# Transformer block on one core: the residual reaches the output by copies and accumulating transfers, operand sums get four places, and the steps of the last down stage are reordered

## The reference

```
h = rms_norm(x, pre_ffn_norm) * (1.0 + sc2) + sh2
u = h @ w_up;  a, b = split(u, 2)
a = causal 3-tap convolution of a, + conv_b
y = (gelu(a) * b) @ w_down            # 5504 -> 2048
out = x + g2 * rms_norm(y, post_ffn_norm)
```

## Time and profile before

| | us |
|---|---|
| median of 3 runs (lowest, highest) | 2706.27 (2702.97, 2706.83) |
| the profiled execution: its time | 2704.7 |
| its span, first to last event | 2703.1 |
| TensorE busy | 2629.2 (97%) |
| VectorE busy | 2077.8 (77%) |
| ScalarE busy | 1158.3 (43%) |
| GpSimd busy | 210.0 (8%) |

### The profile page before, as it was taken

How to read it: one execution, slowest core, us unless ns; L and a number is a source line. 1 busy time by engine, 2 the same in 40 slices (tenths; PEclk the granted TensorE clock), 3 DMA queues, 4 the chain that set the end, 5 groups by cost and what they waited for, 6 DMA issues and landing times.

```text
span 2703.1 us, 40800 instructions
## 1 busy us (share of the span) xinstructions
PE 2629.2 (97%) x14114; PEld 2208.5 (82%) x14114; DVE 2077.8 (77%) x3029; ACT 1158.3 (43%) x1553; POOL 210.0 (8%) x334
## 2 busy tenths in 40 slices
PE   5999999999999999999989999999999998999997
PEld 5788888888788888887878888888888887888886
DVE  7956676666766666626657999999999998888988
ACT  4344444444622222223254444444444444454544
POOL 0030000000000000002200111111111111111000
PEclk8999999999999999999989999999999999999999
DMA  9932322333277777736743665656565566888894
GB/s 362 335 113 85 87 82 81 86 86 86 68 221 217 217 217 217 217 96 234 270 148 94 168 163 128 163 135 159 140 152 147 145 154 218 299 295 310 312 330 149
DMA packets 477847, 485.64 MB, mean 180 GB/s; under 512 B 24603, under 2 KB 381234, under 8 KB 475040
## 3 DMA queue, kind: packets, MB, share of 16 engines
q1 hardware_dynamic: 442160, 384.87, 47.1%
q0 software_dynamic: 25664, 94.93, 11.8%
q10 hardware_dynamic: 9904, 4.26, 0.6%
HBM read 428.28 MB, written 34.75 MB: 171 GB/s over the span
## 4 chain that ended last, share of the span: by engine, by line
PE 90%; DVE 4%; DMA 2%; ACT 2%; issue 1%; SPq 1%; DVEq 0%; POOL 0%; ACTq 0%; POOLq 0%
PE acc_bank L849 14%; PE acc_bank L851 14%; PE acc_bank L850 14%; PE acc_bank L1280 8%; PE acc_bank L1284 4%; PE bank_pb L1280 3%; PE bank_tb L1280 3%; PE bank_ta L1280 3%; PE two_banks L1280 3%; PE two_banks L849 2%; PE two_banks L851 2%; PE two_banks L850 2%; PE two_banks L1284 1%; PE bank_pb L1284 1%; PE bank_tb L1284 1%
## 5 line engine op out<-in xcount | busy, mean ns | idle before, releaser
L840 DVE TENSOR_TENSOR w_lo<-raw,w_hi 128x1024 fp32r<-128x1024 f32 x215 | 263.0, 1224 | 371.5 <-ACT w_hi L834 371.4
L834 ACT CAST w_hi<-raw 128x1024 fp32r<-128x1024 f32 x215 | 225.4, 1049 | 541.6 <-PE acc_bank L851 379.4
L849 PE MATMUL acc_bank<-h_hi,w_hi 128*128 128x512 f32 x1124 | 447.4, 398 | 6.4 <-DVE h_lo L2008 6.4
L851 PE MATMUL acc_bank<-h_hi,w_lo 128*128 128x512 f32 x1124 | 439.1, 391 | 0.0
L850 PE MATMUL acc_bank<-h_lo,w_hi 128*128 128x512 f32 x1124 | 438.8, 390 | 0.0
L849 PEld LDWEIGHTS acc_bank<-h_hi,w_hi 128*128 128x128 f32 x1124 | 211.6, 188 | 50.3 <-issue 6.5
L851 PEld LDWEIGHTS acc_bank<-h_hi,w_lo 128*128 128x128 f32 x1124 | 211.5, 188 | 45.4
L850 PEld LDWEIGHTS acc_bank<-h_lo,w_hi 128*128 128x128 f32 x1124 | 211.8, 188 | 41.8
L1280 PE MATMUL acc_bank<-h_pair,s_hi 128*128 128x512 f32 x640 | 160.3, 392 | 0.0
L1994 DVE SCALAR_TENSOR_TENSOR acc<-raw,csil,acc 128x512 f32<-128x512 f32 x180 | 135.1, 751 | 11.0 <-DMA raw<-in_w_mod_dram 6.5
L1280 PEld LDWEIGHTS acc_bank<-h_pair,s_hi 128*128 128x128 f32 x640 | 115.1, 189 | 20.6
(11 more groups left out here) (730 smaller groups left out, 6355.3 us busy)
## 6 DMA issues: line engine op xcount, KB each, us to landing
raw<-in_w_in_dram SPq DMA_DIRECT2D x148, 512.0 KB, 4.0
raw<-in_w_mod_dram SPq DMA_DIRECT2D x96, 512.0 KB, 4.5
raw<-in_w_ffn_up_dram SPq DMA_DIRECT2D x92, 512.0 KB, 4.9
raw<-in_w_ffn_down_dram SPq DMA_DIRECT2D x86, 512.0 KB, 5.9
raw_odd<-in_w_ffn_up_dram SPq DMA_DIRECT2D x80, 512.0 KB, 5.1
raw_more<-in_w_ffn_down_dram SPq DMA_DIRECT2D x63, 512.0 KB, 6.0
mods_low<-in_w_mod_dram SPq DMA_DIRECT2D x32, 512.0 KB, 10.1
raw<-in_w_out_dram SPq DMA_DIRECT2D x32, 512.0 KB, 4.4
```

Of the source, the lines that this page charges most:

```text
L834: act.copy(w_pair(g, gp)[0][:], raw[n % RAW][:]).then_inc(hi_ready, 1)
L840: dve.tensor_tensor(w_l[:], raw[n % RAW][:], w_h[:].bitcast(F32), ALU.subtract).then_inc(lo_ready, 1)
L849: pe.matmul(o, stat[0], mov[0], start=start, stop=False)
L851: return pe.matmul(o, stat[1], mov[0], start=False, stop=stop)
```

## The change

- The residual no longer passes through SBUF. Where `x2_again` was loaded, GpSimd's queue copies `x2_scr` into `out`, DRAM to DRAM, four rows of 1 MB. Finished rows or half rows are then added to `out` by transfers that accumulate (`accum_op`), on GpSimd's queue. SyncE's final stores go.
- `finish_half` with its residual becomes a multiplication by rms alone: six half rows on ScalarE (`scale_half`), two on VectorE.
- The operand sums have four places in both stages (`u_place`): `op_group_u(g)` waits for the store of group g - 4, and stage 1 loads up to four ahead. The loads wait for the landing of the load before them on the same semaphore.
- `LEFT_B` gets a place of its own (`left_b`), `LEFT_B_AT` goes from 7 to 3 and `LEFT_B_AGAIN` from 12 to 6. The steps of `third_stage`, the squares and the first two roots move to earlier j; the products by the gain all come before the end of stage 3.

The core of the diff (parts left out are marked):

```diff
-LEFT_B_AT = 7
-LEFT_B_AGAIN = 12
+LEFT_B_AT = 3
+LEFT_B_AGAIN = 6
...
-        def u_made(g):
-            return y2[:, 2 + g % 2, 0:512].rearrange("p (k t) -> p k t", k=2)[:, 0:group_tiles(g)[1], :]
-
-        def u_again(g):
-            return y2[:, 2 + g % 2, 512:1024].rearrange("p (k t) -> p k t", k=2)[:, 0:group_tiles(g)[1], :]
+        def u_place(g):
+            c = g // 2 % 2 * 512
+            return y2[:, 2 + g % 2, c:c + 512].rearrange("p (k t) -> p k t", k=2)[:, 0:group_tiles(g)[1], :]
...
-            for i in range(TT + 1):
-                r = ROW_ORDER[min(i, TT - 1)]
-                n, cols = (2 * i + 2, slice(0, D)) if i < TT - 1 else (TT + i, slice((i - TT + 1) * PIECE, (i - TT + 2) * PIECE))
-                sp.wait_ge(out_ready, READY_0 + n)
-                sp.dma_start(out_rows[r][:, cols], y2[:, r, cols]).then_inc(out_stored, 16)
-            sp.wait_ge(out_stored, OUT_0 + 16 * (TT + 1))
...
+            def scale_half(n, half, y):
+
+                i = ROW_ORDER[n]
+                act.wait_ge(scale_ready, SCALE_0 + n + 1)
+                A_(y, y, ACT.Identity, scale=rms[:, i:i + 1]).then_inc(out_ready, 1)
...
+                    if st == 3 and j == 15:
                         y_rms(0)
                         y_rms(1)
...
+                    if st == 3 and j in (18, 19):
+                        n = j - 18
+                        act.wait_ge(b_weighed, 3 + n)
+                        scale_half(n, 0, quarter_row("a1", n))
+                        scale_half(n, 1, quarter_row("b1", n))
...
-                if g > 1:
-                    dve.wait_ge(u_stored[g % 2], U_STORED_0 + 16 * (g // 2))
+                if g > 3:
+                    dve.wait_ge(u_stored[g % 2], U_STORED_0 + 16 * (g // 2 - 1))
...
-            def finish_half(i, half, y):
-                cols = slice(half * PIECE, half * PIECE + PIECE)
-                STT(y2[:, i, cols], y, rms[:, i:i + 1], x2_again[:, i, cols], ALU.mult, ALU.add).then_inc(out_ready, 1)
+            def finish_half(i):
+                dve.wait_ge(scale_ready, SCALE_0 + 3 + i)
+                y = quarter_row("b0", i)
+                TS(y, y, rms[:, i:i + 1], None, ALU.mult).then_inc(quarter_step, 1)
...
-                if j in (4, 5):
                     dve.wait_ge(bank_kept, KEPT_0 + 12)
-                    dve.wait_ge(quarter_step, QUARTER_0 + 2)
-                    for b in (2 * j - 8, 2 * j - 7):
+                    for b in (2 * j - 4, 2 * j - 3):
                         add_bank("p5", 1, "a1", "a1", b)
...
+                if j in (5, 7):
+                    less_second("b0", (j - 5) // 2)
+                if j in (6, 7):
                     dve.wait_ge(quarter_step, QUARTER_0 + 6)
-                    for b in (2 * j - 22, 2 * j - 21):
+                    for b in (2 * j - 12, 2 * j - 11):
                         add_bank("left1", 1, "b1", "b1", b, ALU.subtract)
...
-            for i in ROW_ORDER:
-                pool.dma_start(x2_again[:, i, :], x2_scr[i]).then_inc(back_landed, 16)
+            for i in range(TT):
+                pool.dma_start(out_rows[i], x2_scr[i]).then_inc(back_landed, 16)
+
+            def add_to_out(r, cols, y):
+                pool.dma_start(out_rows[r][:, cols], y, accum_op=ALU.add).then_inc(back_landed, 16)
+
             pool.wait_ge(back_landed, 64)
+            for n in range(2):
+                pool.wait_ge(out_ready, READY_0 + 2 * n + 2)
+                add_to_out(2 + n, slice(0, D), y2[:, 2 + n, :])
+            for i in range(2):
+                pool.wait_ge(quarter_step, QUARTER_0 + 11 + i)
+                if i == 0:
+                    pool.wait_ge(out_ready, READY_0 + 5)
+                    add_to_out(0, slice(0, PIECE), weighed_row[:, 0, :])
+                    add_to_out(0, slice(PIECE, D), y2[:, 0, PIECE:D])
+                else:
+                    add_to_out(1, slice(PIECE, D), y2[:, 1, PIECE:D])
+                    pool.wait_ge(out_ready, READY_0 + 6)
+                    add_to_out(1, slice(0, PIECE), weighed_row[:, 1, :])
+            pool.wait_ge(back_landed, 64 + 16 * 6)
```

More of the change, by code:

```diff
@@ L1922, in _ @@
-                    if st == 3 and j == 17:
+                    if st == 3 and j in (8, 9):
+                        act.wait_ge(bank_added, 8 + 2 * (j - 8) + 2)
+                        square_row(j - 8, "b1", j - 8, 4 * (j - 6) + 2)
+                    if st == 3 and j in (10, 11):
+                        act.wait_ge(quarter_step, QUARTER_0 + j - 1)
+                        square_row(j - 8, "a1", j - 10, 4 * (j - 8) + 1)
+                    if st == 3 and j in (12, 13):
+                        act.wait_ge(bank_added, 12 + 2 * (j - 12) + 2)
+                        square_row(j - 8, "b0", j - 12, 4 * (j - 12) + 2)
@@ new lines, in square_last @@
+            def square_last(i, part):
+                act.wait_ge(y_added, 2 * i + part + 1)
+                act.wait_ge(y2_sq, SQ_0 + 6 + 2 * i + part)
+                A_(op_sum[:, 0].rearrange("p a b -> p (a b)"), y2[:, i, part * 512:part * 512 + 512], ACT.Square,
+                   accum_out=ssg[:, 4 * i + part:4 * i + part + 1]).then_inc(y2_sq, 1)
+            square_last(0, 0)
+            square_last(0, 1)
+            y_rms(2)
+            square_last(1, 0)
+            act.wait_ge(b_weighed, 8)
@@ L1937, in _ @@
+            scale_half(2, 0, weighed_row[:, 0, :])
+            square_last(1, 1)
+            y_rms(3)
+            act.wait_ge(b_weighed, 10)
+            scale_half(3, 0, weighed_row[:, 1, :])
         @block.vector
@@ new lines, in third_stage @@
+                if j in (9, 10):
+                    dve.wait_ge(quarter_step, QUARTER_0 + 8)
+                    for b in (2 * j - 18, 2 * j - 17):
+                        add_bank("left0", 1, "b0", "b0", b, ALU.subtract)
+                if j == 11:
+                    dve.wait_ge(gain_landed, 32)
+                    for i in range(2):
+                        dve.wait_ge(y2_sq, SQ_0 + 1 + i)
+                        weigh_row("b1", i)
+                if j in (12, 13):
+                    i = j - 12
+                    dve.wait_ge(y2_sq, SQ_0 + 3 + i)
@@ L2733, in third_stage @@
                     weigh_row("a1", i)
+                    sum_row(2 + i, 1, 3 + i)
                 if j in (14, 15):
[L2735 to L2742, removed]
-                    root_of(0)
-                    dve.wait_ge(back_landed, 64)
-                    dve.wait_ge(b_weighed, 1)
-                    finish_half(2, 0, quarter_row("a1", 0))
@@ L2819, in _ @@
                         third_stage(j)
[L2821 to L2824, removed]
             def finish_last(b):
@@ L2983, in store_u @@
                     pool.wait_ge(u_stored[g % 2], U_STORED_0 + 16 * (g // 2))
-                pool.dma_start(u_scr[g][:, 0:n, :], u_made(g)).then_inc(u_stored[g % 2], 16)
+                pool.dma_start(u_scr[g][:, 0:n, :], u_place(g)).then_inc(u_stored[g % 2], 16)
             def load_u(st, g):
                 n = group_tiles(g)[1]
-                pool.wait_ge(u_stored[g % 2], U_STORED_0 + 16 * (g // 2 + 1))
-                if g >= 2:
-                    if st == 1:
-                        pool.wait_ge(op_step, op_step_no(1, g - 2, 1))
-                    else:
-                        pool.wait_ge(op_lo_ready, op_no(2, 0, g - 2))
-                pool.dma_start((u_again(g), op_sum[:, g % 2, 0:n, :])[st - 1], u_scr[g][:, 0:n, :]).then_inc(u_landed[g % 2], 16)
+                over = max(n for n in range(OP_GROUPS) if n % 4 == g % 4) if st == 1 else g
+                pool.wait_ge(u_stored[over % 2], U_STORED_0 + 16 * (over // 2 + 1))
+                landed = g // 2 + (st == 2) * ((OP_GROUPS + 1 - g % 2) // 2)
+                if landed:
+                    pool.wait_ge(u_landed[g % 2], U_LANDED_0 + 16 * landed)
+                if st == 1 and g >= 4:
+                    pool.wait_ge(op_step, op_step_no(1, g - 4, 1))
+                if st == 2 and g >= 2:
+                    pool.wait_ge(op_lo_ready, op_no(2, 0, g - 2))
+                pool.dma_start((u_place(g), op_sum[:, g % 2, 0:n, :])[st - 1], u_scr[g][:, 0:n, :]).then_inc(u_landed[g % 2], 16)
             def bring_act(g):
@@ L3021, in _ @@
                 pool.wait_ge(x2_stored[i], 16)
-            load_u(1, 0)
-            load_u(1, 1)
+            for g in range(4):
+                load_u(1, g)
             pool.wait_ge(grow_stored, 32)
@@ L3027, in _ @@
                 store_sum(j)
-                if j % 2 == 0 and j // 2 + 2 < OP_GROUPS:
-                    load_u(1, j // 2 + 2)
+                if j % 2 == 0 and j // 2 + 4 < OP_GROUPS:
+                    load_u(1, j // 2 + 4)
             pool.wait_ge(op_lo_ready, op_no(1, 1, OP_GROUPS - 1))
```

62 lines of the change are left out of this document (22 added, 40 removed).

## The result

Over 12 runs of each the changed kernel takes 2710.68 us (2709.22 to 2712.35) and the one before 2705.47 (2702.97 to 2707.95): ratio 1.0021, 95% interval 1.0012 to 1.0029. The change costs 5.2 us; the forecast was 6.1 us less, 2700.2, and 2710.7 lies above its range. The profiled execution took 2709.22 us, with a span of 2707.6, 4.5 us more than before's 2703.1.

A forecast was written before the change was run, and what follows sets the result against it. TensorE holds 90% of the chain, so time could come only from its waits and the stretch after its last matmul. Stage 0 -6.4, stall +0.5, end -0.2: -6.1 from 2706.27 gives 2700.2 us, range 2698.3 to 2702.5.

The forecast's parts named there:

- The end: After the last matmuls: engines finish 6 us earlier, but accumulating transfers take this back, leaving 0.2 us gained.
- T: Start of the four kept pieces near the kernel's end, 2677.90 in the trace before; times of the end count from it.
- the one of the other side: Rival at the end: read, add and write in DRAM do not overlap, 15.6 us more, 2715.8, slower; 13%.
- Stage 0: Four places remove VectorE's wait for a store; TensorE's gap shrinks to 2.1 us, clock stays 1.00; 6.4 us gained.
- `LEFT_B` again: Stage 3: TensorE waits for VectorE's additions to banks 2 and 3, a stall of 0.5 us, bounds 0 and 2.7.
- The copy: Stage 3: copying into out costs nothing; a rival had it starve the weights, 4 us, 2704.2; 4%.
- The last bank: At the end: piece 20 is 0.4 us late where 1.2 was lost before, so the bank is full at T + 11.4.
- The price a: Time of an accumulating transfer into DRAM at the end: 2.86 us per 512 KB, bounds 1.28 and 4.14.
- both rivals of a dearer accumulation: At the end: 3.3 to 4.4 us per 512 KB, 2708.9 at 4.14, 13%; or 5.0 us without overlap, 2715.8, 13%.
- the one of a = 1.28: Rival at the end: accumulation costs no more than a store, engines set the end at T + 18.9, 2694.1; 12%.
- The last landing: At the end: row 0 asked for at T + 11.8, four halves take 11.4 us, last lands at T + 25.0.
- The signal that I named: Sign of a wrong prediction: last engine idle more than 11 us before the end, meaning a larger price a.

The follow-up runs named there:

- no_pool_drain: The changed kernel with its block closed without GpSimd's drain, GpSimd still waiting for the landings; 2703.84 us, ratio 0.9995 to the kernel before.
- pool_waits_last: The kernel before with one wait more: GpSimd too waits until SyncE's output stores have landed; 2711.17 us, ratio 1.0023 to the kernel before.
- wait_on_sync: The changed kernel with the last wait, for the accumulating transfers' landings, moved from GpSimd to SyncE; 2707.14 us, ratio 1.0008 to the kernel before.
- places_alone: The kernel before with only the operand sums' four places and the loads that go with them; 2700.87 us, ratio 0.9982 to the kernel before.
- last_rows_by_dve: The changed kernel with rows 0 and 1 given their residual by VectorE and stored by SyncE, which waits for everything; 2697.89 us, ratio 0.9976 to before.
- steps_and_adds: The changed kernel with the operand sums in their two places again; 2714.86 us, ratio 1.0037 to the kernel before.
- plain_stores: The changed kernel with plain stores for the six accumulating transfers, so its output lacks the residual; 2703.45 us, ratio 0.9992 to the kernel before.
- last_rows_filled: last_rows_by_dve with eight small matmuls adding zero in the first of TensorE's two stage 0 gaps; 2698.23 us, ratio 0.9974 to the kernel before.

## Why the prediction was wrong

The step that failed is the last one of **The end**: "rows 0 and 1 are four halves, 11.4 us, so the last lands at T + 13.0 + 11.4 + 0.6 = T + 25.0. Before it was T + 25.2: **0.2 us gained**". It takes the last landing for the end of the span. That was nearly right before, where SyncE waited for it (0.4 us). In the changed kernel GpSimd waits, and its drain puts 7.7 us behind the landing. `no_pool_drain` removes it, `pool_waits_last` makes it appear in the kernel before, `wait_on_sync` halves it. None of my rivals had this term: the one of the other side asked for dearer accumulations. The length was to be had from before's trace, where GpSimd's drain at 2635.0 shows its 6.8 us; I read only views that leave it out.

Point by point, from the profiled executions. The sum: forecast -6.1, measured +4.5 by the spans. Counted from the fixed matmul above, and so without the 0.8 us that the execution was ahead, it is +5.3, as the medians have it (+5.2); that leaves 11.4 us to account for.
- **Stage 0**, forecast -6.4. The gap was right (2.1 us). The new wait on group 3's blocks came on VectorE (0.96 us), but TensorE, for which 0.4 was priced, did not notice it. The mis-sized part is "I price the forms at 2.72": the clock fell all the same, 12.67 us for four forms, 1.8 lost. That the granted clock was 1.00 at the moment of resuming did not say that it would stay. From the fixed matmul on the stage gives 4.2 (about -6.4 + 1.8 - 0.4 + 0.7, the last for the late form ahead), the runs of `places_alone` 4.1.
- **`LEFT_B` again**, forecast +0.5: measured 0.32. Right place, right releaser. T came 4.37 us earlier by the span and 3.6 from the fixed matmul, where 5.9 was forecast: 2.3 of the 11.4.
- **The copy**, forecast 0: right; loads beside it were slower, and TensorE noticed nothing.
- **The last bank**, forecast full at T + 11.4: its last matmul starts at T + 11.7 and ends at T + 12.1 (before, T + 12.3). The wait on `kept_lo` stayed at 0.71, not 0.4. The last transfer is asked for at T + 15.9 (forecast T + 15.0).
- **The price a**, forecast 2.86: measured 2.91 (2.95 to 3.00 in the runs that end alike). The nearest row, an accumulation on chip, carried over into DRAM; the bound of 4.14 and both rivals of a dearer accumulation fell, and so did the one of a = 1.28.
- **The last landing**, forecast T + 25.0: measured T + 26.3 (up to T + 27.8 in the runs that end alike). Row 0 is asked for at T + 12.4 (forecast T + 11.8), and its data start at T + 13.8 (forecast T + 13.0). The four halves then take 12.2 us, 3.06 each of DMA time, where 11.4 was forecast (rows 2 and 3 took 2.76 each). This is 1.3 of the 11.4.
- **Landing to end**, forecast 0: measured 7.7. With the 2.3 and 1.3 this makes 11.3, the 11.4 within rounding.

With this term added the forecast would have said -6.1 + 7.7 = +1.6 us, within 0.2% of before. The other misses, 2.3 and 1.3 us, would have stayed; they have the same sign and do not cancel. The signal that I named, more than 11 us of idle engines before the end (ScalarE's last operation ends at 2689.03, 18.6 us before it), did come; its cause was not a larger a.

## What to carry to other kernels

A kernel is over when its slowest engine has ended, not when its data have landed. Look in the trace for what each engine does behind its last instruction, and give the last wait to an engine whose end is cheap; keep transfers that only GpSimd can issue for data that is ready well before the end. An edit that is right in its parts can be worth splitting: here the places gave 4 us, the new order with the early additions some 3 more (fixed matmul to the end of the span: 445.3 us in `places_alone`, 441.7 in `last_rows_by_dve`; no run splits this part further), and the last two rows' transfers with one wait on GpSimd turned it into a loss.

## What the runs showed of the hardware that I had not expected

- GpSimd's drain at the end takes 6.80 us in the kernel before, where it starts 0.2 us behind the landing of its queue's last transfer, and 6.80 us in `pool_waits_last`, where it starts 68 us behind it. In the changed kernel, `steps_and_adds` and `plain_stores`, which end with six transfers to the output, plain or accumulating, it takes 7.30 us. Entered before the last landing, it ends 3.5 to 3.6 us after it (`last_rows_by_dve`, `wait_on_sync`). Why half of it can overlap, and why it is 6.80 or 7.30, is open. The end of SyncE's program took 0.4 us from landing to span end. The Trainium skill (VectorE: DVE Perf Modes, The DRAIN you can't avoid) gives the drains of a program's preamble and postamble as some 12 ns on all five engines. The drains at the start of these traces are of that size on four engines (7 to 10 ns) and take 0.19 us on GpSimd. The one that the kernel's own block puts at GpSimd's end, and that `no_pool_drain` leaves out, is not: 6.80 or 7.30 us.
- Accumulating into DRAM: 2.91 us per 512 KB in all 16 engines, 180 GB/s, against 1.30 for plain stores from the same queue. The Trainium skill (Collectives: The Full Stack, The bandwidth ceiling) gives a ratio of two between copy and reduction; the runs give 2.2.
- In the changed kernel the granted clock fell to 0.50 1.6 us after TensorE had resumed, for some 3.4 us, behind a gap of only 2.1 us that followed one of 1.4. In `last_rows_filled` the gap ahead was closed and the clock fell behind the one of 2.04 us all the same, 1.2 us after TensorE had resumed. With small matmuls of 64 rows by 128 columns in that gap it stayed at 1.00, in both traces that have them, one of which still has a gap of 2.09 us ahead.
